# Two turnings of a feed-forward placed inside its third group's products, and the last attention's value weights split one piece ahead

## The reference

```
# first model, layer 0 (m = 0) and layer 1 (m = 1)
y = _short_conv_mixer(x, ...)            # m = 0
y = _mla_mixer(x, ...)                   # m = 1, 8 heads, latent keys and values
x = _layer_norm(ALPHA * x + y, ln_mix_g[i], ln_mix_b[i])
x = _layer_norm(ALPHA * x + _sq_relu_mlp(x, ff_w1[i], ff_w2[i]), ln_ff_g[i], ln_ff_b[i])

def _sq_relu_mlp(x, w1, w2):
    return jnp.square(jax.nn.relu(x @ w1)) @ w2        # 1024 -> 4096 -> 1024

# second model: a gated recurrence, then an attention with shared keys and values
h = _modulate(_rmsnorm(x, norm_g[layer]), shift, scale)
y = _rglru_mixer(h, ...)                 # layer 0
k_sh, v_sh, km_sh = _shared_kv(x, cs, kv_norm_g, kv_mod_w, kv_mod_b, w_kv)
y = _moba_mixer(h, k_sh, v_sh, km_sh, att_w_in, att_w_out)   # layer 1
x = x + gate[:, None, :] * y
```

## Time and profile before

| | |
|---|---|
| median of 3 runs | 780.31 us (780.28 to 780.37) |
| profiled execution, its own time | 780.2 us |
| its span, first to last instruction | 778.4 us |
| TensorE busy | 768.9 us, 99% of the span, granted clock 0.998 |
| VectorE / ScalarE / GpSimd busy | 586.1 / 405.1 / 34.6 us |
| HBM | 172.10 MB read, 222 GB/s over the span |

### The profile page before, as it was taken

The page is one execution under the profiler, slowest core; times in us unless marked ns, Lnnn a source line. Parts: engine busy times, 40 slices in busy tenths (PEclk is TensorE's granted clock), DMA queues, the critical chain, the costliest instruction groups (busy, mean ns, idle before and its releaser), DMA issues.

```text
span 778.4 us, 12084 instructions
## 1 busy us (share of the span) xinstructions
PE 768.9 (99%) x4982; PEld 697.1 (90%) x4982; DVE 586.1 (75%) x786; ACT 405.1 (52%) x512; POOL 34.6 (4%) x66
## 2 busy tenths in 40 slices
PE   9999999999999999999999999999999999999996
PEld 9999888988998889888889988998799988999995
DVE  5886898868688697687989776676687877756754
ACT  5455235545445424875355444445649869664632
POOL 0000000000000001000000000000500051000001
PEclk9999999999999999999999999999999999999999
DMA  9877438897867731446488977876235254754102
GB/s 351 319 274 278 184 125 324 348 320 289 313 231 288 290 122 62 163 139 267 165 326 344 347 273 275 308 263 245 103 109 216 109 216 163 270 216 164 55 3 80
DMA packets 26983, 173.94 MB, mean 223 GB/s; under 512 B 3248, under 2 KB 3632, under 8 KB 7856
## 3 DMA queue, kind: packets, MB, share of 16 engines
q1 hardware_dynamic: 26640, 173.14, 60.0%
q10 hardware_dynamic: 288, 0.02, 0.0%
HBM read 172.10 MB, written 1.05 MB: 222 GB/s over the span
## 4 chain that ended last, share of the span: by engine, by line
PE 93%; DVE 3%; ACT 2%; POOL 1%; issue 0%; POOLq 0%; ACTq 0%
PE bank L578 12%; PE bank L580 12%; PE bank L579 12%; PE Y L714 10%; PE Y L716 10%; PE Y L713 10%; PE bank L1067 2%; PE bank L1068 2%; PE bank L1069 2%; PE bank L996 2%; DVE w_low L1610 1%; PE bank L816 1%; PE Y L738 1%; PE bank L610 1%; PE bank L619 1%; PE bank L611 1%
## 5 line engine op out<-in xcount | busy, mean ns | idle before, releaser
L1610 DVE TENSOR_TENSOR w_low<-raw,w_high 128x2048 fp32r<-128x2048 f32 (+3 forms) x125 | 278.5, 2238 | 65.1 <-ACT w_high L1203 62.8
L1203 ACT CAST w_high<-raw 128x2048 fp32r<-128x2048 f32 (+3 forms) x125 | 232.5, 1869 | 92.9 <-DMA raw<-weights 80.0
L578 PE MATMUL bank<-xT_h,w_high 128*128 128x256 f32 x728 | 206.5, 284 | 0.1
L579 PE MATMUL bank<-xT_l,w_high 128*128 128x256 f32 x728 | 205.8, 283 | 0.0
L580 PE MATMUL bank<-xT_h,w_low 128*128 128x256 f32 x728 | 205.8, 283 | 0.0
L578 PEld LDWEIGHTS bank<-xT_h,w_high 128*128 128x128 f32 x728 | 139.4, 192 | 1.6 <-DVE w_low L1610 0.3
L579 PEld LDWEIGHTS bank<-xT_l,w_high 128*128 128x128 f32 x728 | 139.4, 191 | 1.1
L580 PEld LDWEIGHTS bank<-xT_h,w_low 128*128 128x128 f32 x728 | 139.5, 192 | 0.0
L714 PE MATMUL Y<-w_low,hT_h 128*128 128x512 f32 x324 | 128.3, 396 | 0.0
L713 PE MATMUL Y<-w_high,hT_h 128*128 128x512 f32 x324 | 128.0, 395 | 0.0
L716 PE MATMUL Y<-w_high,hT_l 128*128 128x512 f32 x324 | 101.9, 395 | 0.0
(11 more groups left out here) (291 smaller groups left out, 1144.5 us busy)
## 6 DMA issues: line engine op xcount, KB each, us to landing
raw<-weights SPq DMA_DIRECT2D x149, 1024.0 KB, 5.0
rows<-rows_in SPq DMA_DIRECT2D x9, 512.0 KB, 7.7
raw<-weights SPq DMA_DIRECT2D x4, 576.0 KB, 3.5
z<-gates_in SPq DMA_DIRECT2D x4, 512.0 KB, 3.8
raw<-weights SPq DMA_DIRECT2D x2, 896.0 KB, 4.4
raw<-weights SPq DMA_DIRECT2D x3, 512.0 KB, 7.0
x<-x_in SPq DMA_DIRECT2D x2, 512.0 KB, 4.4
kT<-rows_in SPq DMA_DIRECT2D x2, 512.0 KB, 8.3
```

Of the source, the lines that this page charges most:

```text
L578: mm(dst, high, xh[:, kt, :], start=kt == 0, stop=False)
L579: mm(dst, high, xl[:, kt, :], start=False, stop=False)
L1203: nc.scalar.copy(w_high[:, n % RING, start:COLS[n]], raw[:, s % RAW, start:COLS[n]]).then_inc(w_high_ready, 1)
L1610: tt(w_low[:, n % RING, start:COLS[n]], slot[:, start:COLS[n]], f32(w_high[:, n % RING, start:COLS[n]]), ALU.subtract).then_inc(raw_done, 1)
```

## The change

In `feed_forward` of TensorE's program, the third group's 24 products of each token block are cut in two halves of 12 (input tiles 0 to 3 and 4 to 7). The first half of block 0 now stands ahead of the turning of x, and the first half of block 1 ahead of `turn_pair(phase, 0)`. Both feed-forwards run this function. In ScalarE's and VectorE's programs the splits of v1, v2 and v3 around "rs2" stand one place earlier: ScalarE casts v2 ahead of the squares of token block 0, and v3 behind that block's modulation; VectorE splits v1 ahead of the gated residual of block 0, v2 behind the wait for the root, and v3 behind the residual of block 1.

```
--- before.py
+++ after.py
@@ -743,12 +743,14 @@
 
                 first = [open_unit(phase, g) for g in range(FILL)]
                 pair_block(first[0], phase, 0, fresh)
+                up_block(first[2], PI[phase, "up", 2], 0, fresh, range(0, KT // 2))
                 transposes(fresh, x, "x_ready", [1])
-                up_block(first[2], PI[phase, "up", 2], 0, fresh)
+                up_block(first[2], PI[phase, "up", 2], 0, fresh, range(KT // 2, KT))
                 pair_block(first[1], phase, 1, fresh)
+                up_block(first[2], PI[phase, "up", 2], 1, fresh, range(0, KT // 2))
                 turn_pair(phase, 0)
                 in_order(phase, 2)
-                up_block(first[2], PI[phase, "up", 2], 1, fresh).then_inc(product, 1)
+                up_block(first[2], PI[phase, "up", 2], 1, fresh, range(KT // 2, KT)).then_inc(product, 1)
                 turn_pair(phase, 1)
                 for g in range(FILL, FFG):
                     for b in range(TB):
@@ -1501,7 +1503,7 @@
                 act.wait_ge(rg_hidden, i + 1)
                 hidden_high_of("rg", i)
                 split_ahead([("rg", "g", 3), ("rg", "down", 0), ("rg", "down", 2), ("rg", "down", 3)][i], 0)
-            split_ahead(("rg", "down", MXG - 1), 2)
+            split_ahead(("rg", "down", MXG - 1), 3)
             rms_squares("rs2", "rg", 0)
             rms_scale("rs2", 0)
             def gate_kept(n):
@@ -1510,10 +1512,9 @@
                 nc.scalar.copy(z[:, 0, n * 512:(n + 1) * 512], bank_of("gate", 1, n)[:, :]).then_inc(evacuates("gate", 1, n), 1)
 
             scaled_transposed("rs2kv", 0, *modulation["rs2kv"])
-            split_ahead(("rg", "down", MXG - 1), 3)
+            split_ahead(("rg", "down", MXG - 1), 4)
             gate_kept(0)
             rms_squares("rs2", "rg", 1)
-            split_ahead(("rg", "down", MXG - 1), 4)
             rms_scale("rs2", 1)
             gate_kept(1)
             scaled_transposed("rs2kv", 1, *modulation["rs2kv"])
@@ -2032,10 +2033,10 @@
                     split_ahead(("rg", "down", 3), 0)
                 hidden_low_of("rg", i)
                 split_ahead([("rg", "g", 2), ("rg", "g", 3), ("rg", "down", 1), ("rg", "down", 3)][i], 0)
-            split_ahead(("rg", "down", 3), 1)
+            split_ahead(("rg", "down", 3), 2)
             gated_residual("rg", 0, 0)
             await_rstd("rs2", 0)
-            split_ahead(("rg", "down", 3), 2)
+            split_ahead(("rg", "down", 3), 3)
             split_transposed("rs2kv", 0, *modulation["rs2kv"], [0])
             gated_residual("rg", 0, 1)
             split_ahead(("rg", "down", MXG - 1), 4)
```

## The result

The changed kernel takes **781.8 us** in the median of 18 executions (780.85 to 782.39), the kernel before 780.32 us beside it (779.82 to 781.21). The ratio is 1.0018, with a 95% interval of 1.0011 to 1.0024: slower by 1.5 us between the medians, by 0.9 to 1.9 us over the interval. The forecast was 781.2, slower by 0.9, with 10% for more than 0.2%. The measured time lies inside the stated range (779.9 to 782.0), by 0.2 us, and just outside the forecast's own case (780.8 to 781.6).

The account below looks back on a forecast made before the run. TensorE, busy for 99% of the span, was taken as the bound, so only its waits count. +0.43 + 0.77 - 0.30 = +0.90 us on 780.2 gives 781.1, plus 0.1 for the median: 781.2 us; range 779.9 to 782.0.

Parts of the forecast that it names:

- the forecast's own case: Whole kernel: the forecast holds with a time of 780.8 to 781.6 us; chance 60%.
- Second feed-forward, what goes: Turning of x in the second feed-forward: the waits for VectorE's layer norm go, a gain of 0.84 us on TensorE.
- Second feed-forward, what comes: Second feed-forward: VectorE's row behind the turning runs late to token block 1's hT_l, and TensorE waits; net +0.77 us.
- First feed-forward: First feed-forward: nothing is won at the turning, and VectorE's row shifts until block 1's hT_l holds up TensorE; net +0.43 us.
- The other turning: turn_pair of block 0 in the first feed-forward: moving it by 1.44 us is free, by 0.15 us.
- The values: Around rs2: v2's wait of 0.33 us goes, late GpSimd columns and scaling cost 0.03; net -0.30 us.
- the split of v1 will hold up the next one in the same way: GpSimd's columns around rs2: VectorE's split of v1 delays another column instruction, so the last column ends 1.7 us later.
- The sum: Whole kernel: +0.43 + 0.77 - 0.30 = +0.90 us, forecast 781.2 us, 0.1% slower.
- The late landing of v2: ScalarE's cast of v2 ahead of the squares: a late load delays the squares by 1.4 us, total 782.3; chance 8%.
- Both prices in the feed-forwards: Rival that VectorE catches up in one feed-forward, so one of two losses is not paid: 780.4 to 780.8; chance 12%.
- VectorE did not wait for GpSimd: Rival around rs2: v1's split waits up to 0.6 us for a GpSimd column instruction, total 781.5; chance 12%.
- All is won: Rival that VectorE's lateness is covered in both feed-forwards, giving 0.84 and 0.30: 779.2 us; chance 8%.

Follow-up runs that it names:

- the first and third experiments: Against the kernel before: first, both product moves with the splits around rs2 unmoved, 781.93 against 780.53; third, only the turning of x moved, 781.42 against 780.53.
- the ninth experiment: The changed kernel with VectorE's late splits, four gate columns on ScalarE, and group 3's activation ahead of one split; 1.6 us faster than the kernel before.
- the fastest kernel: The kernel of the ninth experiment, with executions from 778.14 to 779.94 us.

## Why the prediction was right, and which terms were off

**Second feed-forward, what goes: right.** 0.84 us forecast. The turning has no idle time and lasts 1.03 us; when nothing else was late the head fell from 25.22 to 24.35, 0.87.

**Second feed-forward, what comes: right, with its parts.** +0.77 forecast, +0.75 measured, in the changed kernel and in the first and third experiments. The waits forecast for it, about 0.7 for the square and 0.6 at the thirteenth `down` product, are 0.67 and 0.58 when read from the starts (0.51 and 0.42 in brackets). The prediction named VectorE's work in between incompletely: besides two modulation pieces and two splits there are three squares and the `hT_l` of block 0. The sum doesn't use the list, only that there is no idle time in it.

**First feed-forward: right.** +0.43 forecast, +0.48 measured. The shift of VectorE's row was 1.26 us against 1.23. The thirteenth product is 0.38 us late and the one behind it 0.10 more, a part that the forecast didn't count.

**The other turning: right as part of the sum, wrong if read alone.** Costed at nothing beside the turning of x, and it adds little there: 0.11 us in the first head (24.85 with both, 24.74 with x alone), nothing in the second (25.96 and 25.97). The room of 0.15 us that the prediction gave it on TensorE is 0.2 by its own terms. Alone it costs 0.95 us in the two heads. The text named the reason, that two more steps are queued behind it, but not that it would be a price of its own without the other move. It also does something the prediction didn't see: it keeps TensorE from a wait of 1.02 us for the square.

**The values: mis-sized, the one term with the wrong sign.** -0.30 forecast, +0.06 in the changed kernel's stage. The 0.33 us of v2 went as forecast. The step that failed is "the split of v1 will hold up the next one in the same way": the prediction let GpSimd's instruction pass between the splits of v0 and v1 and be held by one split only. It was held through both, 4.52 us instead of twice about 2.4, so the columns ended 2.1 us late instead of 1.7, the root 0.60 instead of 0.21 us late. The prediction gave a sign for this, a scaling more than 0.3 us late against the residual, and it is 0.59 late (644.61 - 639.68 against 641.89 - 637.55). The slack was smaller too: TensorE starts 0.11 us after the first half is reckoned ready (644.61 + 0.67 = 645.28, then 645.39), so of the 0.28 us only 0.17 were free. 0.60 - 0.17 = 0.43 is what the turning is late by. At the first value TensorE is 0.49 behind, and where v2's wait was it comes back to 0.06. The mechanism stands: with the columns shared the stage gives 0.43 us less than before the change.

The trace of the kernel before already showed such a double hold, in the column ahead of the one in the earlier trace rows, which the prediction didn't read:

```profile
630.42 3.10 POOL L1135 TENSOR_SCALAR rows<-ones,modcol 128x128 f32<-128x128 f32 x1 [66.01 <-DVE buf_b L2030]
```

```profile
630.25 2.28 DVE L1610 TENSOR_TENSOR w_low<-raw,w_high 128x2048 fp32r<-128x2048 f32 x1
632.45 0.68 DVE L1626 TENSOR_TENSOR hT_l<-buf_b,hT_h 128x512 fp32r<-128x512 f32 x1
```

It took 3.10 us, through a split and the `hT_l` right behind it, and ended 0.39 us after the second.

**The sum.** +0.90 forecast, +1.31 by stages, +1.48 between the medians; 0.36 of the 0.41 by stages is this term.

**The rivals.** The late landing of v2, whose 782.3 is as near to the measured time as the forecast, did not occur: the cast ended 0.24 us ahead of the squares. Both prices in the feed-forwards were paid. VectorE did not wait for GpSimd: its two splits took 4.58 us together where the port's rule as the prediction applied it would have added up to 0.6. As to the rule itself (the Trainium skill, SBUF — State Buffer, Who interferes with whom), the trace agrees that GpSimd is shut out while the split holds the port, 4.52 against 0.60 us; no run here shows VectorE held for a whole instruction. "All is won" was not the changed kernel, but the kernel of the ninth experiment is that case made true, by taking VectorE's cover from elsewhere.

## What to carry to other kernels

When work is put ahead of a step that feeds another engine, the wait it hides is one side; the other is that this engine's whole row of work behind the step starts later by as much, up to its next idle time. Follow that row to the last thing that TensorE reads from it before costing the move. When a move that should win doesn't, look at what the helper does between the fed step and the step that is read, and put that work behind it, but then check what is queued behind the loads that now start late: here the gain of 0.84 us reached the executions only with all three, the placings, the late splits, and the activation ahead of a split. And read a loss from the starts, for the idle time shown beside it can be less (0.51 for 0.67 us here, 1.02 for 1.17).

## What was not expected of the hardware

- **An instruction of GpSimd can be shut out through two VectorE instructions in a row.** With one split beside it a column instruction took 2.40 us; with two splits back to back it took 4.52 us, with a split and a `hT_l` 3.10 us, and 0.60 with none of these. It was 4.52 us in the trace of the splits alone as well.
- **The start of the program varies.** In the profiles the first product of the first feed-forward stands at 101.59 us before the change, at 102.46 in the changed kernel and at 101.00 in the fastest kernel, and the second block of the input `x_in` landed at 6.67, 7.75 and 6.28 us. A single profiled span can so be off by as much as the change under study, while the stages of these traces repeat within 0.15 us where nothing was changed. The span in the changed kernel's profile, 780.6 against 778.4, overstates the change by 0.87 us for this reason.
